# A decoder block on one core: the first expert phase in 22 steps instead of 43, with more of the first tile's rows in the mixer

## The reference

```python
q = jnp.einsum('bsd,dk->bsk', h, w_q).reshape(b, s, PEER_HEADS, 2, PEER_DKEY // 2)
scores = jnp.einsum('bshcd,hcnd->bshcn', q, sub_keys).astype(jnp.float32)
s1, i1 = lax.top_k(scores[..., 0, :], PEER_TOPK)
s2, i2 = lax.top_k(scores[..., 1, :], PEER_TOPK)
...
top_s, pos = lax.top_k(cand, PEER_TOPK)
ids = jnp.take_along_axis(cand_ids, pos, axis=-1)
gates = jax.nn.softmax(top_s, axis=-1)
...
act = jax.nn.gelu(jnp.einsum('td,tkd->tk', hx, u_tab[idx]), approximate=False) * g
return jnp.einsum('tk,tkd->td', act, v_tab[idx])
```

## Time and profile before

| | |
|---|---|
| median of 3 runs | 3636.15 us (3626.55 to 3640.84) |
| the profiled execution | 3633.03 us, span 3631.3 us |
| mean granted TensorE clock | 0.881 |
| busy: PE, DVE, POOL, ACT | 81%, 54%, 44%, 15% of the span |
| DMA | 981.5 MB, 270 GB/s in the mean |

### The profile page before, as it was taken

The page is one execution under the profiler, slowest core; times in us unless marked ns, Lnnn a source line. Parts: engine busy times, 40 slices in busy tenths (PEclk is TensorE's granted clock), DMA queues, the critical chain, the costliest instruction groups (busy, mean ns, idle before and its releaser), DMA issues.

```text
span 3631.3 us, 31990 instructions
## 1 busy us (share of the span) xinstructions
PE 2954.5 (81%) x10195; PEld 1466.3 (40%) x10195; DVE 1948.0 (54%) x4610; ACT 557.6 (15%) x1043; POOL 1580.0 (44%) x1444
## 2 busy tenths in 40 slices
PE   8999988884425545556399999999999999999997
PEld 3455545542214313333144444444444444444443
DVE  2335434684799677866475656455565544441113
ACT  1321133221004402444110000000000000000000
POOL 0010001241455365576336666655567666553331
PEclk9999979887766677666699999999999999999998
DMA  3000202332875597777779999999999999997883
GB/s 111 34 24 24 83 26 87 125 109 98 320 293 187 185 408 283 269 267 275 306 278 403 409 398 417 400 360 417 380 383 409 389 417 410 409 378 277 314 311 136
DMA packets 307573, 981.52 MB, mean 270 GB/s; under 512 B 29904, under 2 KB 57680, under 8 KB 306640
## 3 DMA queue, kind: packets, MB, share of 16 engines
q0 software_dynamic: 184320, 671.17, 48.1%
q1 hardware_dynamic: 120464, 307.85, 22.2%
q10 hardware_dynamic: 2624, 0.46, 0.1%
HBM read 941.63 MB, written 37.75 MB: 270 GB/s over the span
## 4 chain that ended last, share of the span: by engine, by line
PE 34%; DMA 12%; POOL 12%; issue 7%; DVE 6%; ACT 2%; DVEq 0%; ACTq 0%; SPq 0%; POOLq 0%
PE part L1659 10%; PE hid L1640 10%; DMA v_ring<-in_peer_v_dram,ids_t 9%; POOL u_ring L1578 6%; PE acc L1687 5%; POOL v_ring L1587 5%; PE turn_ps L1631 4%; PE part L1668 3%; DVE u_ring L1947 2%; DMA gate_grid<-room 2%; POOL dense_sums L1608 1%; ACT dense_sums L1728 1%; DMA u_ring<-in_peer_u_dram,ids_u 1%; DMA keys_pair<-in_peer_keys_dram 1%; ACT dense_sums L1726 0%
## 5 line engine op out<-in xcount | busy, mean ns | idle before, releaser
L1947 DVE CUSTOM_DVE_ANT_0 u_ring<-u_ring,x_rows_in 128x1024 f32<-128x1024 f32 x608 | 743.0, 1239 | 472.4 <-DMA u_ring<-in_peer_u_dram,ids_u 456.1
L1587 POOL DMA_INDIRECT v_ring<-in_peer_v_dram,ids_t x640 | 674.4, 1054 | 605.2 <-PE acc L1687 422.5
L1578 POOL DMA_INDIRECT u_ring<-in_peer_u_dram,ids_u x608 | 676.9, 1113 | 449.6 <-DVE dots L1947 276.7
L1640 PE MATMUL hid<-x1t_dense,dense_u 128*128 128x384 f32 x2048 | 698.4, 495 | 1.2 <-issue 1.2
L1659 PE MATMUL part<-room,weights 128*128 128x512 f32 x1536 | 682.7, 594 | 9.2 <-DMA room<-in_peer_v_dram 8.9
L1640 PEld LDWEIGHTS hid<-x1t_dense,dense_u 128*128 128x128 f32 x2048 | 383.7, 192 | 338.4 <-issue 103.4
L1687 PE MATMUL acc<-v_ring,line 128*32 128x512 f32 x2560 | 348.7, 668 | 118.0 <-DMA v_ring<-in_peer_v_dram,ids_t 117.8
L1659 PEld LDWEIGHTS part<-room,weights 128*128 128x128 f32 x1536 | 291.1, 191 | 352.8 <-issue 325.1
L1668 PE MATMUL part<-dense_sums 128*128 128x128 f32 x768 | 175.4, 405 | 241.4 <-ACT dense_sums L1728 130.9
L1755 ACT ACTIVATE weights<-hid 128x384 f32<-128x384 f32 x128 | 62.8, 490 | 1463.8 <-PE hid L1640 1463.8
L1918 DVE TENSOR_TENSOR dense_sums<-dense_sums,part 128x512 f32<-128x512 f32 x186 | 126.6, 685 | 254.2 <-PE part L1659 253.8
(11 more groups left out here) (312 smaller groups left out, 2588.7 us busy)
## 6 DMA issues: line engine op xcount, KB each, us to landing
wq_pair<-in_peer_wq_dram SPq DMA_DIRECT2D x32, 2048.0 KB, 14.7
dense_u<-in_peer_ut_dram SPq DMA_DIRECT2D x128, 512.0 KB, 7.0
room<-in_peer_v_dram SPq DMA_DIRECT2D x128, 512.0 KB, 8.7
gate_grid<-room SPq DMA_DIRECT2D x6, 4096.0 KB, 15.8
room<-gate_grid SPq DMA_DIRECT2D x32, 768.0 KB, 18.0
w_ring<-in_w_in_dram SPq DMA_DIRECT2D x5, 2048.0 KB, 7.9
v_ring<-in_peer_v_dram,ids_t POOLq DMA_INDIRECT x640, 9.3
u_ring<-in_peer_u_dram,ids_u POOLq DMA_INDIRECT x608, 9.2
```

The costliest lines, as they stand in the source:

```text
L1578: pool.indirect_dma_start(u_ring[:, n % U_RING, :], None, peer_u, bass.IndirectOffsetOnAxis(ap=ids_u[:, q, k:k + 1], axis=0))\
L1587: pool.indirect_dma_start(v_ring[:, n % V_RING, :], None, peer_v, bass.IndirectOffsetOnAxis(ap=ids_t[:, q % 2, token:token + 1], axis=0))\
L1640: last = mm.matmul(hid[:, 0:DT], ud[:, c % UD_RING, k, :], x1td[:, k, :], start=(k == 0), stop=(k == KC - 1))
L1947: vec.tensor_tensor_reduce(u_ring[:, n % U_RING, :], u_ring[:, n % U_RING, :], x1[:, q % 2, :], 1.0, 0.0, ALU.mult, ALU.add, dots[:, q % 2 ...
```

## The change

The order of the expert block is written anew. A dense tile's or gathered tile's pairs stand one a step instead of one in two steps in steps 0 to 15 (tiles 1, 2, 4, 3), a dense tile's groups are 8 in each of 4 steps, and V quads of tile 0 are up to 4 a step in steps 6 to 14. `DENSE_AT` is 22 instead of 43. In steps 6 to 13 a pair, 8 groups and 4 quads (2 in step 6) stand together; steps 0 to 5 and 13 to 28 have 8 U rows each. 80 instead of 32 U rows of tile 0 are in the mixer, four a step in its steps 22 to 41. From step 29 on each step has a chunk, 4 U rows and one quad; from 125 to 140 two quads and no U row; 141 to 149 a chunk alone. Token groups are held three at a time for two, the stage has two buffers for one (the room is shared with the rings of the dense phase, so the first three dense U chunks are now loaded at step 20, after the fifth stage is stored, and the affine vectors after the first V chunks). Within a step the work is interleaved: DVE and GpSimd in 8 parts, PE and ACT in 4 quarters. `weigh` follows one step behind a tile's last U row for two, and V quads one step behind for three. The tiles are chosen in the order 1, 2, 4, 3 instead of 1, 4, 2, 3.

```diff
@@ -40,6 +40,7 @@
...
+FIRST_SLOTS = 5 * TOPK
...
         roped = sb("roped", [P, 2, ATT], to=scan)
...
         sq = sb("sq", [P, SSD], to=scan)
...
-                return (2, 2, 3, 4)[k % DA_HEADS]
+                return 4
...
 DT = ND * P
-CHOSEN_AT = {1: 0, 4: 8, 2: 16, 3: 24, 5: 40, 6: 54, 7: 86}
-PAIR_STEPS = {1: 2, 4: 2, 2: 2, 3: 2, 5: 2, 6: 6, 7: 6}
+CHOSEN_AT = {1: 0, 2: 4, 4: 8, 3: 12, 5: 17, 6: 36, 7: 68}
+PAIR_STEPS = {1: 1, 2: 1, 4: 1, 3: 1, 5: 3, 6: 6, 7: 6}
 TURN_ORDER = (0, *CHOSEN_AT)
 PAIRS = HEADS // 2
-DENSE_AT = 43
+DENSE_AT = 22
 BLOCK = 4
 BLOCKS = NKEYS // BLOCK
 STEPS = DENSE_AT + NKEYS + BLOCK + 1
-U_AT = (0, 17, 50, 82, 114)
-U_EACH = (6, 4, 4, 4, 4)
-U_BASE = (0, 96, 224, 352, 480)
-V_AT = (18, 51, 84, 116, 148)
-LAST_V = (48, 81, 114, 146, 171)
+PARTS = 8
+QUARTERS = 4
+U_AT = (0, 13, 29, 61, 93)
+U_EACH = (8, 8, 4, 4, 4)
+U_BASE = (0, 48, 176, 304, 432)
+V_COUNTS = ((2, 4, 4, 4, 4, 4, 4, 4, 2), (2,) + 30 * (1,), (2,) + 30 * (1,), (2,) + 30 * (1,), 16 * (2,))
+V_AT = (6, 29, 61, 93, 125)
+LAST_V = tuple(at + len(counts) - 1 for at, counts in zip(V_AT, V_COUNTS))
+NORM_AT = (24, 60, 92, 124, 141)
 U_RING = 5
 V_RING = 8
...
@@ -1242,11 +1247,16 @@
 QUADS = P // 4
 LINE_QUADS = 4
 LINES = QUADS // LINE_QUADS
-TOKEN_STEPS = 8
+TOKEN_STEPS = 4
+HELD = 3
 GROUPS = ND * P // 4
...
+
+def share(items, i, n):
+
+    return items[i * len(items) // n:(i + 1) * len(items) // n]
 
...
 
+def choosing(step, part):
+
+    last, before = chosen_pair(step - 1), chosen_pair(step - 2)
+    if last is not None and step - 1 < DENSE_AT and part % 2:
+        return part // 2, *last
+    if last is not None and step - 1 >= DENSE_AT and part in (1, 4):
+        return part // 3, *last
+    if before is not None and step - 2 >= DENSE_AT and part in (1, 4):
+        return 2 + part // 3, *before
+    return None
+
...
     for q, t in enumerate(GATHERED):
-        last = CHOSEN_AT[t] + (PAIRS - 1) * PAIR_STEPS[t] if t else -2
-        if step == (last + 5 if q < 2 else max(last + 5, LAST_V[q - 2] + 2)):
+        if step == (chosen_step(t) + 2 if q < 2 else max(chosen_step(t) + 2, LAST_V[q - 2] + 2)):
             return q
     return None
...
     for d, t in enumerate(DENSE):
-        x = step - (CHOSEN_AT[t] + (PAIRS - 1) * PAIR_STEPS[t] + 5)
+        x = step - (chosen_step(t) + 2)
         if 0 <= x < TOKEN_STEPS:
-            return [d * QUADS + 4 * x + i for i in range(4)]
+            each = QUADS // TOKEN_STEPS
+            return [d * QUADS + each * x + i for i in range(each)]
     return []
 
...
-            else:
-                at = x + 1 if x else 0
-                count = 1 if x else 2
-            return [(q * QUADS + s, q, s) for s in range(at, at + count)]
+        if 0 <= x < len(V_COUNTS[q]):
+            at = sum(V_COUNTS[q][:x])
+            return [(q * QUADS + s, q, s) for s in range(at, at + V_COUNTS[q][x])]
...
         x1td = sb("x1t_dense", [P, KC, DT])
         sums_d = sb("dense_sums", [P, ND, D])
...
-        std = sb("std2", [P, 1])
-        tmp = sb("tmp2", [P, 1])
+        small = sb("norm_columns", [P, 16])
+        stats = small[:, 0:12].rearrange("p (h k) -> p h k", h=2)
+        mv, rstd, var, std, tmp = small[:, 12:14], small[:, 0:1], small[:, 14:15], small[:, 15:16], small[:, 1:2]
         ends = top[:].rearrange("p c k -> p (c k)")
         stats_d = ends[:, 0:12 * ND].rearrange("p (d h k) -> p d h k", d=ND, h=2)
         mv_d = ends[:, 12 * ND:14 * ND].rearrange("p (d k) -> p d k", d=ND)
         var_d, std_d, rstd_d, tmp_d = (ends[:, (14 + i) * ND:(15 + i) * ND] for i in range(4))
 
-        stage = room[:, 0:NKEYS * STAGE_TOKENS].rearrange("p (i n) -> p i n", n=STAGE_TOKENS)
+        stages = [room[:, i * NKEYS * STAGE_TOKENS:(i + 1) * NKEYS * STAGE_TOKENS].rearrange("p (i n) -> p i n", n=STAGE_TOKENS)
+                  for i in (1, 0)]
         vd = room[:, 0:VD_RING * D].rearrange("p (r d) -> p r d", d=D)
-        gates_d = room[:, VD_RING * D:].rearrange("p (r z i n) -> p r z i n", r=2, z=STAGES, i=BLOCK)
-        spare = weights[:].rearrange("p c i n -> p (c i n)")
-        parts = spare[:, 0:2 * SLOTS].rearrange("p (c k) -> p c k", c=2)
-        parts_t = spare[:, 2 * SLOTS:2 * SLOTS + 6 * P].rearrange("p (d c n) -> p d c n", d=2, c=3)
-        is_i2 = sums_d[:, 0, :].rearrange("p (k j n) -> p k j n", k=2, j=4)
-        is_i1 = sums_d[:, 1, :].rearrange("p (k j n) -> p k j n", k=2, j=4)
+        at_gates, at_u, at_weights = VD_RING * D, VD_RING * D + 2 * BLOCK * DT, VD_RING * D + 2 * BLOCK * DT + UD_RING * D
+        ud = room[:, at_u:at_weights].rearrange("p (r c n) -> p r c n", r=UD_RING, c=KC)
+        weights = room[:, at_weights:].rearrange("p (r i n) -> p r i n", r=2, i=BLOCK)
+        gates_d = room[:, at_gates:at_u].rearrange("p (r z i n) -> p r z i n", r=2, z=STAGES, i=BLOCK)
+        g2, b2 = affine[:, 0, :], affine[:, 1, :]
+        spare = affine[:].rearrange("p c n -> p (c n)")
+        parts = spare[:, 0:4 * SLOTS].rearrange("p (d c k) -> p d c k", d=2, c=2)
+        parts_t = spare[:, 4 * SLOTS:4 * SLOTS + 6 * P].rearrange("p (d c n) -> p d c n", d=2, c=3)
+        marks = sums_d[:].rearrange("p d n -> p (d n)").rearrange("p (c k j n) -> p c k j n", c=2, k=HELD, j=4)
+        is_i2, is_i1 = marks[:, 0, :, :, :], marks[:, 1, :, :, :]
 
         acc = [ps(f"acc{h}", [P, 512]) for h in range(2)]
...
         group_kept = sem("group_kept_e")
-        stage_stored = sem("stage_stored_e")
...
                     sp.wait_ge(hid_done, c - UD_RING + 1)
+                else:
+                    sp.wait_ge(stage_stored[0], STAGES // 2 * 16)
                 sp.dma_start(ud[:, c % UD_RING, :, :].rearrange("p c n -> p (c n)"), peer_ut[c * P:(c + 1) * P, :])\
                     .then_inc(ud_landed[c % UD_RING], 16)
 
             def load_v(c):
                 if c < VD_RING:
-                    sp.wait_ge(stage_stored, STAGES * 16)
...
-                    sp.wait_ge(stage_stored, STAGES * 16)
+                    for i in range(2):
+                        sp.wait_ge(stage_stored[i], STAGES // 2 * 16)
                 sp.dma_start(gates_d[:, n % 2, :, :, :].rearrange("p s c n -> p s (c n)"),
...
             load_x1(1)
-            sp.dma_start(g2[:], ln2_g.partition_broadcast(P)).then_inc(ln2_in, 16)
-            sp.dma_start(b2[:], ln2_b.partition_broadcast(P)).then_inc(ln2_in, 16)
-            for c in range(UD_RING):
-                load_u(c)
             for s in range(STEPS):
                 for k in token_groups(s):
                     z, i = divmod(k, STAGE_TOKENS // 4)
                     if i == STAGE_TOKENS // 4 - 1:
                         sp.wait_ge(group_kept, k + 1)
-                        sp.dma_start(g_dram[z].rearrange("p i n -> p (i n)"), stage.rearrange("p i n -> p (i n)"))\
-                            .then_inc(stage_stored, 16)
+                        sp.dma_start(g_dram[z].rearrange("p i n -> p (i n)"), stages[z % 2].rearrange("p i n -> p (i n)"))\
+                            .then_inc(stage_stored[z % 2], 16)
                         if z == STAGES - 1:
                             load_gates(0)
                             for d, t in enumerate(DENSE):
@@ -1534,6 +1560,11 @@
                             load_gates(1)
                             for c in range(BLOCK, VD_RING):
                                 load_v(c)
+                            sp.dma_start(g2, ln2_g.partition_broadcast(P)).then_inc(ln2_in, 16)
+                            sp.dma_start(b2, ln2_b.partition_broadcast(P)).then_inc(ln2_in, 16)
+                if s == DENSE_AT - 2:
+                    for c in range(UD_RING):
+                        load_u(c)
                 c = dense_chunk(s)
                 if c is not None:
...
                 rows, quads = u_rows_at(s), quads_at(s)
-                if rows and rows[0][2] == 0:
-                    pool.wait_ge(tiles_chosen, list(CHOSEN_AT).index(GATHERED[rows[0][1]]) + 1)
-                if quads and quads[0][2] == 0:
-                    pool.wait_ge(ids_t_ready, quads[0][1] + 1)
-                for i in range(max(len(rows), 4 * len(quads))):
-                    if i < len(rows):
-                        gather_u(*rows[i])
-                    if i < 4 * len(quads):
-                        gather_v(*quads[i // 4], i % 4)
-                for k in token_groups(s):
-                    d, at = k // QUADS, (k % QUADS) * 4
-                    pool.wait_ge(parts_t_ready, d + 1)
-                    if k >= 2:
-                        pool.wait_ge(group_built, k - 1)
-                    pool.tensor_tensor(is_i2[:, k % 2, :, :], iota[:].unsqueeze(1).broadcast_to([P, 4, P]),
-                                       parts_t[:, d % 2, 1, at:at + 4].unsqueeze(2).broadcast_to([P, 4, P]), ALU.subtract)\
-                        .then_inc(from_i2_ready, 1)
+                v_rows = [(*quad, j) for quad in quads for j in range(4)]
+                for i in range(PARTS):
```

(37 more changed lines are left out.)

357 lines of the change are left out of this document (168 added, 189 removed).

## The result

The changed kernel took 3703.64 us (median; 3698.35 to 3717.42), the kernel before 3638.49 in the same session: ratio 1.019, 95% interval 1.0152 to 1.0228. The forecast was 3597 with a range to 3685; the time lies outside it and on the other side of no change. The profiled execution has a span of 3704.4 us, 112 above the forecast's 3592 and 73 above the 3631 of before. One execution among the experiments, of e8, took 3866.63 us at a granted clock of 0.804 where its others had 0.88; it fell into a slower state of the chip and is left out.

The account below looks back on a forecast made before the run. The order of dependent work was taken to bound the first expert phase; PE and DMA were nearly full in the dense phase. 3631 + 33 (mixer) - 82 (first phase) - 10 (start) + 20 (rest) = 3592 span, 3597 median; range 3505 to 3685.

Parts of the forecast that it names:

- The new layouts of buffers, of small columns and of semaphores cost nothing: they add no instruction.: Whole kernel: the changed placement of buffers, small columns and semaphores in memory was entered at no cost.
- Steps 7 to 13 at 48 us: First expert phase: a pair, 8 groups and 4 quads take 48 us a step, stage stores included.
- the 54 at which the gain was said to be gone: Expert steps 7 to 13: at 54 us a step the change would no longer gain.
- Steps 125 to 140 at 16 us: Late dense steps with two quads: 16 us each, between 14.4 and 17.3, 256 us in all.
- the rest: From step 29 to the end: 1756 us, against 1736 from step 50 before, so +20.
- Mixer +33: Mixer's end: 48 more U rows make it end at about 932 instead of 899; bounds +5 and +58.
- Steps 0 to 5 at 25 us: Start of the expert block: one pair and 8 rows take 25 us a step, set by DVE.
- Start 133 us to step 29: Start of the dense phase: 133 us from chunk 0 to step 29, against 143 to step 50 before.
- Packs well: Rival: steps 7 to 13 take about 40 us, the mixer's tail hides more; about 3523 us; chance 0.25.
- Dense phase takes it back: Rival: coefficients lie on PE's path, 9 us at each of four tiles, +36, about 3633 us; chance 0.13.
- Added up: Rival: groups and gathers don't overlap, 64 us a step, +112, about 3709 us; chance 0.12.
- GpSimd's contention: Rival: GpSimd's operations take their longest times beside DVE's reductions, +93, about 3690 us; chance 0.05.

Follow-up runs that it names:

- e8: The changed kernel with 48 U rows in the mixer instead of 80, and 16 in each of steps 0 to 4: 3696.24 us, 1.0171.
- e13: The changed kernel, 80 mixer rows kept, with e4, e7 and e11 together: 3568.98 us, 0.9827.
- e4: The changed kernel with the next pair's weights and keys asked for ahead of the wait for a stage's last group and its store: 3645.32 us, 1.0018.
- e7: The changed kernel with the last tile's 32 V quads over 24 steps (2, 1, 1) instead of 16 steps of 2: 3663.16 us, 1.0064.
- e11: The changed kernel with a small tile allocated first, so its rings lie 64 bytes further on, at a multiple of 256: 3677.72 us, 1.011.
- e12: The kernel before with its rings and all behind them moved by 160 bytes: 3678.94 us, 1.0123.
- e14: The kernel before with its rings and all behind them moved by 128 bytes: 3672.31 us, 1.01.
- e15: The kernel before with its rings and all behind them moved by 64 bytes: 3677.13 us, 1.0107.
- e9: The changed kernel with 32 mixer rows, 16 in each of steps 0 to 5, plus e4 and e7: 3570.61 us, 0.9821.
- e10: The changed kernel with the products of the mixer's 80 U rows cut to 64 of 1024 columns, rows fetched as before: 3662.49 us, 1.0066.
- e6: The changed kernel with the four later gathered tiles' coefficients and V rows two steps later: 3696.05 us, 1.015.
- e3: The changed kernel with 32 U rows in the mixer as before, and 16 in each of steps 0 to 5: 3669.75 us, 1.0099.
- e5: The changed kernel with e3 and e4 together: 3611.51 us, 0.993.
- e17: The kernel of e13 with the mixer's weights, keys and U ring also starting at a multiple of 256 bytes: 3573.97 us, 0.9818.
- e16: The kernel before with rings and dense U chunks kept, the tiles behind them (V chunks, gates, token rows) 64 bytes on: 3643.03 us, 1.0015.
- e18: The kernel before with the U ring kept, the V ring and all behind it 64 bytes on: 3652.3 us, 1.0051.

## Why the prediction was wrong

The idea that was forecast to gain does gain: with three side costs taken away the same plan takes 3569.0 us (e13), 70 less than before, more than the 41 forecast. The costs are 58 (e4), 40 (e7) and 26 (e11), 125 together; 3703.6 less 125 is 3579, and 3569 was measured. But the forecast isn't borne out term by term: e13's five stretches differ from the kernel before by +65, -111, +10, -19 and -9 us, where the forecast had +33, -82, -10, 0 and +20. The 19 us in the 96 steps were not forecast, and no run gives their reason; that the plan gains at all is shown, that it gains more than 41 is in part luck.

- **"The new layouts of buffers, of small columns and of semaphores cost nothing: they add no instruction."** This step failed in kind. Forecast 0, measured 26 us (e11), and 33 to 40 on the kernel before (e12, e14, e15), of which 24 to 30 in the 96 steps. The first dot products grew by 192 bytes, and the rings of gathered rows went from a multiple of 256 to 192 past one. So +4 in the 96 steps is no "same": e9 and e13, whose rings start at a multiple of 256, take 1339 and 1340 us there.
- **Steps 7 to 13 at 48 us, "9 to 15 more every second step" for the store.** The mechanism was seen, its size was not. Without a store a step takes 43 to 46 us; a step with a store ahead of the weights takes 19 to 25 more than the same step in e4. The mean of steps 7 to 13 is (1566.7 - 1164.1) / 7 = 57.5 us, past the 54 at which the gain was said to be gone, and 67 us in all above the 336 of the forecast. e4 takes it away with one change of order, 83 us by step 14, of which 60 are left at chunk 0: steps 14 to 21 take 230 us in e4, close to the 233 of the forecast, and 207 in the changed kernel, which so hides 23 of what steps 7 to 13 cost. The estimate was 15.8 us for the store and 7 for the weights, less 8 that were counted already; from the store to the matmul it was 29.0, with 11.0 of them spent issuing the keys, and the 27 us that SP had already held the weights back, waiting for the stage's last group, were not in the estimate.
- **Steps 125 to 140 at 16 us.** Measured 17.7, above the upper end of the 14.4 to 17.3: 283 us for 256. The term "the rest" was +20 and came out at +39. e7, with one or two quads a step instead of always two, takes 46 us off that stretch.
- **Mixer +33.** It was +74. At least 36 of it is not VectorE's work on the rows (e10), and VectorE's waits for landings point to the ring of four. The prediction's bounds, 5 to 58, were left behind, since both counted VectorE's time alone. But the step's real error is that it was entered in the sum at all beside steps 0 to 5: e13 and e9 end alike, so 48 rows more or less at the mixer's end are worth nothing here.
- **Steps 0 to 5 at 25 us.** Right: VectorE's first instructions for a pair begin 24.4 to 26.2 us apart, 25.0 in the mean.
- **Start 133 us to step 29.** Chunk 0 to step 30 took 161, 8 more than before instead of 10 less. PE stood 37.0 us for the fourth dense U chunk. That wait was expected in kind; that it would cost more than the start of before, was not. Of the named risk, the affine loads, SP's queue shows only 2.9 us; the last V loads ahead of them hold it for 17.7. No other order of these loads was tried, so what the wait is worth stays open.
- **The rivals.** *Packs well* had 40 us for the steps and the sum 48; once the store is out of the way they take 45.5 in the mean (e4), between the two. *Dense phase takes it back*: the wait for coefficients is there, once, 18.4 us, and 0.6 in all of 2000 to 3150, not 9 at each of four tiles; e6, which was to remove it, put a like wait in its place. *Added up* gave 3709 and the kernel took 3704, but not by that mechanism (e4); that the number fits is chance. *GpSimd's contention*: medians of a gather are 941 ns for 940 before, of a group 1049 for 1044:

```profile
L1609 POOL DMA_INDIRECT u_ring<-in_peer_u_dram,ids_u x560: 935/941/1988, 968.3 to 3262.9; - x187
...
L1640 POOL TENSOR_TENSOR dense_sums<-iota,affine x96: 1040/1049/1907, 1120.6 to 1762.9; 128x512 f32<-128x512 f32 x96
```

Open: why e11's 96 steps took 1348 us and not the 1331 to 1341 of e3, e5, e9, e13 and e17; what the U ring alone costs; and whether a ring of five or more would give the mixer's landings back, which wasn't tried.

## What to carry to other kernels

Work that is moved along one engine from one busy stretch to the next may be worth nothing, however large the shift that the first stretch shows (59 us here, and 2 at chunk 0); price it at the next point where both orders meet. In a queue that is worked off in order, put small loads that an engine is about to need ahead of a large store that nobody waits for, and ahead of the wait for what it stores (58 us here). And where DMA is the bound, look at the byte at which a gathered tile starts before and after an edit that only changes the size of a small tile: 192 bytes cost this kernel 26 us.

## What the runs showed of the hardware that was not expected

**The start of gathered rows in SBUF.** With the rings of gathered rows (4 KB for each partition) and the tiles behind them 64, 128, 160 or 192 bytes past a multiple of 256, a packet of the gathers takes 148.1 to 148.7 ns for 144.8 to 145.8, and the DMA engines' plateau falls from 417 to 420 down to 404 to 410 GB/s. The V chunks' 512 KB loads and the gates' loads showed nothing of it (e16), and the V ring and the dense U chunks little (e18: 145.8 ns, 3 us in the 96 steps). The Trainium skill (DMA: Bandwidth & Descriptors, How a descriptor splits into AXI transactions) says that a descriptor is cut into transactions of 256 bytes which must start at a multiple of 256, so that one that starts elsewhere can have more of them; it says so of reads, and here the rows are written. By that rule a row of 4096 bytes has 17 for 16, and an estimate from its beats is 2 to 6 on 128, growing with the offset. The direction agrees with the packets where both rings are off. The size does not grow with the offset as the beats do (148.3 at 64 bytes, 148.1 at 128, 148.7 at 160 and at 192), and neither e16's tiles nor e18's V ring follow the rule. So it is not shown to be the cause.

**VectorE beside GpSimd.** Two rows' reductions in the mixer take 3.37 and 3.35 us where 1.22 is the median, while GpSimd multiplies and adds 128x1024 tiles (VectorE, then GpSimd, both in the changed kernel):

```profile
828.61 3.37 DVE L1115 CUSTOM_DVE_ANT_0 u_rows<-u_rows,x_first 128x1024 f32<-128x1024 f32 x1
...
831.91 3.35 DVE L1115 CUSTOM_DVE_ANT_0 u_rows<-u_rows,x_first 128x1024 f32<-128x1024 f32 x1
```

```profile
827.51 3.38 POOL L856 TENSOR_TENSOR x<-x,g 128x1024 f32<-128x1024 f32 x1
831.07 3.10 POOL L858 TENSOR_TENSOR x<-x,b 128x1024 f32<-128x1024 f32 x1 [0.18 <-POOLq L857]
```

Eight of the 80 rows are slowed, and each stands beside one of these GpSimd instructions. They in turn take 2.7 to 3.4 us there, and 2.3 where no row holds them up. The row ahead of the two, at 827.46, took 1.23 us although GpSimd's record begins at 827.51: it looks as if one waits for the other's whole instruction. So the contention that the prediction put on GpSimd's gathers falls on VectorE's reductions, and beside GpSimd's arithmetic. The Trainium skill (GPSIMD Engine Reference, Specifications) has the two share their SBUF interfaces when VectorE's instruction has two SBUF inputs, and the trace agrees with that.
